# Two orders for the long and the short products in the FFN up-projection of a two-block transformer kernel

## The reference

```python
D_MODEL = 2048; SEQ = 256; D_FF = 5632; CONV_WIDTH = 3

def conv_ffn(h, w_up, conv_w, conv_b, w_down):
    B, S, _ = h.shape
    up = h @ w_up                      # [256, 2048] @ [2048, 11264]
    up_p = jnp.pad(up, ((0, 0), (CONV_WIDTH - 1, 0), (0, 0)))
    c = conv_b + sum(conv_w[j] * up_p[:, j:j + S] for j in range(CONV_WIDTH))
    gate, val = jnp.split(c, 2, axis=-1)
    return (jax.nn.silu(gate) * val) @ w_down

def reference(x, ...):
    x = first_block(x, ...)            # ends with x + conv_ffn(rmsnorm(x, ffn_norm_g), ...)
    return second_block(x, ...)
```

## Time and profile before

| | |
|---|---|
| time, median of 3 runs | 2346.7 us (2346.58 to 2346.95) |
| the profiled execution, its own time | 2346.09 us |
| its span, first to last instruction | 2343.8 us |
| TensorE matmul busy | 2329.4 us, 11,306 matmuls |
| TensorE weight load busy | 1944.9 us, 11,306 loads |
| DVE, ACT, POOL busy | 1527.5, 1134.4, 48.4 us |
| mean granted TensorE clock | 0.998 |
| HBM read | 431 MB, 185 GB/s over the span |

### The profile page before, as it was taken

One profiled execution on the slowest core, in us unless ns is written; L12 is line 12 of the kernel. 1 busy time (PEld: TensorE's weight loads), 2 busy tenths in 40 slices (PEclk: granted clock), 3 DMA queues, 4 the chain that ended last, 5 costly groups with the idle time before them and its releaser, 6 DMA issues.

```text
span 2343.8 us, 31449 instructions
## 1 busy us (share of the span) xinstructions
PE 2329.4 (99%) x11306; PEld 1944.9 (83%) x11306; DVE 1527.5 (65%) x1937; ACT 1134.4 (48%) x1418; POOL 48.4 (2%) x61
## 2 busy tenths in 40 slices
PE   9999999999999999999999999999999999999998
PEld 8788888888888888888888888888888888888886
DVE  5567576867777777668656666677656456456557
ACT  6444545644445555544454444455444434444443
POOL 1000000000000000000100000000000000000000
PEclk9999999999999999999999999999999999999999
DMA  9556545555655555565699659955755655665644
GB/s 318 162 171 205 162 152 180 189 190 190 191 190 190 191 188 192 188 191 183 215 177 188 179 172 172 182 183 188 214 171 176 195 167 175 198 188 161 196 156 143
DMA packets 220441, 434.74 MB, mean 185 GB/s; under 512 B 13392, under 2 KB 13680, under 8 KB 219568
## 3 DMA queue, kind: packets, MB, share of 16 engines
q1 hardware_dynamic: 218256, 422.50, 60.8%
q0 software_dynamic: 1648, 10.50, 1.2%
q10 hardware_dynamic: 432, 0.30, 0.0%
HBM read 431.05 MB, written 2.11 MB: 185 GB/s over the span
## 4 chain that ended last, share of the span: by engine, by line
PE 98%; DVE 1%; ACT 0%; DMA 0%; issue 0%; SPq 0%; DVEq 0%; ACTq 0%
PE acc L530 77%; PE mix L530 19%; PE mix L602 0%; PE mix L680 0%; DMA raw<-in_w_in 0%; PE mix L946 0%; PE mix L968 0%; PE mix L696 0%; DVE w_lo L1541 0%; PE mix L711 0%; DVE res L1554 0%; ACT w_hi L1048 0%; DVE res L2245 0%; ACT heads L1048 0%; ACT y_hi L1048 0%
## 5 line engine op out<-in xcount | busy, mean ns | idle before, releaser
L1541 DVE TENSOR_TENSOR w_lo<-raw,w_hi 128x1024 fp32r<-128x1024 f32 x788 | 960.6, 1222 | 585.5 <-ACT w_hi L1048 580.9
L1048 ACT ACTIVATE w_hi<-raw 128x1024 fp32r<-128x1024 f32 (+1 forms) x793 | 836.4, 1057 | 821.4 <-PE acc L530 638.5
L530 PE MATMUL acc<-w_hi,x_both 128*128 128x512 f32 x3296 | 1059.3, 395 | 0.9 <-DVE w_lo L1541 0.6
L530 PEld LDWEIGHTS acc<-w_hi,x_both 128*128 128x128 f32 x3296 | 618.9, 188 | 133.7 <-issue 5.1
L530 PE MATMUL acc<-w_lo,x_both 128*128 128x512 f32 x1648 | 641.7, 389 | 0.0
L530 PEld LDWEIGHTS acc<-w_lo,x_both 128*128 128x128 f32 x1648 | 309.9, 188 | 62.4 <-issue 1.4
L530 PE MATMUL acc<-w_hi,y_hi 128*128 128x512 f32 x640 | 253.6, 396 | 2.2 <-DVE y_lo L1705 2.1
L530 PE MATMUL acc<-x_both,w_hi 128*128 128x512 f32 (+2 forms) x768 | 254.9, 385 | 0.0
L530 PE MATMUL acc<-w_hi,y_lo 128*128 128x512 f32 x640 | 249.4, 390 | 0.0
L530 PE MATMUL acc<-w_lo,y_hi 128*128 128x512 f32 x640 | 249.2, 389 | 0.0
L530 PE MATMUL mix<-x_both,w_hi 128*128 128x512 f32 x704 | 244.5, 394 | 0.0
(11 more groups left out here) (213 smaller groups left out, 1474.1 us busy)
## 6 DMA issues: line engine op xcount, KB each, us to landing
raw<-in_ret_w_in SPq DMA_DIRECT2D x192, 512.0 KB, 4.2
raw<-in_w_up SPq DMA_DIRECT2D x176, 512.0 KB, 3.6
raw<-in_fox_w_in SPq DMA_DIRECT2D x128, 512.0 KB, 5.4
raw<-in_w_down SPq DMA_DIRECT2D x88, 512.0 KB, 4.2
raw<-in_w_in SPq DMA_DIRECT2D x79, 512.0 KB, 3.6
raw<-in_ret_w_out SPq DMA_DIRECT2D x64, 512.0 KB, 3.8
raw<-in_w_out SPq DMA_DIRECT2D x32, 512.0 KB, 3.7
raw<-in_fox_w_out SPq DMA_DIRECT2D x32, 512.0 KB, 4.1
```

Source lines behind the costliest of these rows:

```text
L530: return nc.tensor.matmul(o, l, r, start=start, stop=stop)
L1048: return nc.scalar.activation(o, i_, f, **kw)
L1541: V.tensor_tensor(lo, raw[:, g.base % RAW, :], hi, ALU.subtract).then_inc(lo_done, 1)
```

## The change

In each half chunk the four long products are issued in a row and the four short ones in a row. In chunk 0, where the bank has to be opened by a long product, the long ones come first, in all other chunks the short ones. Within a row the order is tile by tile, and in a tile both groups. The last product of the half chunk, whatever its kind, is the one that carries the semaphore.

```diff
@@ -835,16 +835,16 @@
                         if c == 0:
                             for blk in free[half != FFN_B % 2]:
                                 block_out(pe, blk)
-                        for k in range(KC):
-                            kt = c * KC + k
-                            for f in (2 * half, 2 * half + 1):
-                                at = slice(k * COL + f * P, k * COL + (f + 1) * P)
-                                o = banks[:, f, :].rearrange("p (a s) -> p a s", a=2)
-                                if kt > 0:
-                                    mm(o[:, 0, :], w_lo[:, slot, at], x_hi[:, kt, :], False, False)
-                                done = mm(o, w_hi[:, slot, at], x_both[:, :, kt, :], kt == 0, kt == KT - 1)
-                                if kt == 0:
-                                    mm(o[:, 0, :], w_lo[:, slot, at], x_hi[:, kt, :], False, False)
+                        for long in ((True, False) if c == 0 else (False, True)):
+                            for k in range(KC):
+                                kt = c * KC + k
+                                for f in (2 * half, 2 * half + 1):
+                                    at = slice(k * COL + f * P, k * COL + (f + 1) * P)
+                                    o = banks[:, f, :].rearrange("p (a s) -> p a s", a=2)
+                                    if long:
+                                        done = mm(o, w_hi[:, slot, at], x_both[:, :, kt, :], kt == 0, kt == KT - 1)
+                                    else:
+                                        done = mm(o[:, 0, :], w_lo[:, slot, at], x_hi[:, kt, :], False, False)
                     done.then_inc(used, 1)
                     if build and c + 4 < 8:
                         xt(1, c + 4)
```

## The result

| | before | after |
|---|---|---|
| time, median of 18 runs each | 2346.68 us | 2351.28 us |
| lowest and highest | 2345.92, 2347.14 | 2350.70, 2351.89 |
| ratio | | 1.0020, 95% interval 1.0014 to 1.0027 |
| span of the profiled execution | 2343.8 us | 2349.0 us |

The change costs 4.6 us. The forecast was 2348.8, 2.1 us more than before, with a range up to 2356.1. The sign and the range held; the size was a little over double, and the point lies just at the bound of 0.2% (4.7 us).

The account below looks back on a forecast made before the run. TensorE, never waiting in the FFN, was taken to bound the kernel. 352 half chunks at 6 ns add 2.1 us to the 2346.7 median, giving 2348.8 us; whole range 2343.5 to 2356.1, own range 2346.7 to 2351.3.

Parts of the forecast that it names:

- What bounds it: FFN stretch: TensorE busy for all of 662.1 us, so each nanosecond between two products is a nanosecond of the kernel.
- That nothing else moves: Whole kernel: same products, loads, waits and DMAs; semaphore move and neighbours' different PSUM banks costed at nothing; down blocks stay 21.78 us.
- Short to short at 117, short to long at 115: Column blocks: three short-to-long distances of 115 ns become short to short at 117, adding 6 ns a half chunk.
- Long to long at 232: Column blocks: two-piece long products in a row stand 232 ns apart, as long to short did; ends 227 and 236.
- The sum: All 352 half chunks of the column blocks: 6 ns each, +2.1 us, all on the path.
- three-plus-three formula: Per half chunk of a column block: change is 3 x (LL - LS) + 3 x (SS - SL), LS 232, SL 115.
- my own case: Column blocks: +2.1 us, limited by the first chunk's 13 ns a half chunk; 0.60 together with "The order doesn't matter".
- every change of length disturbs: Column blocks: each run of four never settles, costing 27 ns a half chunk, +9.4 us, 2356.1 us; chance 0.27.
- loads fall behind: Runs of four shorts: 188 ns loads exceed the 115 ns distance; without overlap 219 ns a half chunk, +77 us; chance 0.02.
- like the down blocks: Column blocks: longs in a row go at 227, shorts stay 115, gaining 5.3 us, 2341.4; gain over 4.7 us 0.11.
- The order doesn't matter: Column blocks: each product costs its columns and a fixed 13.4 ns, so 2346.7 stays; 0.60 together with the own case.

Follow-up runs that it names:

- runs of two: Against the kernel before, each tile issues two short products, then two long ones (first tile long first); 2348.54 us, ratio 1.0008.
- runs of eight: The change's order with the second half of each chunk but first and last turned round: eight longs, then eight shorts in a row; 2349.51 us, ratio 1.0012.
- 384 columns in turn: Order of the kernel before, with the short product given 384 columns instead of 256, read from other data; 2438.72 us, one run.

## Why the prediction was right or wrong

*What bounds it.* Right. TensorE never waits in the stretch read, and what its products are apart is what the kernel takes: the column blocks grew by 4.4 us, the median by 4.6.

*That nothing else moves.* Right: no wait was added, the down blocks kept their time, and the banks, tried by themselves in the alternation, cost nothing.

*Short to short at 117, short to long at 115.* Mis-sized. In rows both are 118 to 119, and shorts alone settle at 120. The working took the distance before a long product as one that stays while its neighbours change. In fact the mean of a short record went from 277 to 281, 4 ns on all four distances of a half chunk, where I had 2 ns on three.

*Long to long at 232.* Right as a number (233.2), wrong as a reason. I took 232 as what the two-piece form costs; the run with long products alone shows 226.7 for it. The 233 is a disturbance that a run of shorts leaves behind and that five longs wear off. That it comes out near 232 is chance.

*The sum.* 6 ns a half chunk was forecast and 14 measured; this is the step that failed. The three-plus-three formula by neighbours gives 3 x 1.2 + 3 x 3.6 = 14 with the distances of the kernel after, but the edges it left alone moved too (228.7 for 232, 118.2 for 115), and the same sum by neighbours gave 22.38 us a block for runs of two, which took 22.31, and 22.46 for runs of eight, which took 22.35. The 14 ns are the mean over a block: its steady chunks lost 16 to 17 a half chunk, the first one hardly anything (2780 or 2804 ns a chunk, from 2797 or 2800). The measured rate is close to that of the first chunk, 26 ns in 16 products, which I had in hand and set as the limit of my own case; that the two agree may be luck, as nothing shows one cause for both. And 352 x 14 ns would be 4.9 us; the third block, slow before, took 0.15 us less.

*The rival "every change of length disturbs".* Its mechanism is what happened, at half its price: 27 ns a half chunk was worked out, 14 came. I had each of two changes cost 13. Against the settled prices the longs pay, behind the shorts, and the shorts pay nothing over their 120, often less. Against the kernel before it reads the other way round, as its uneven alternation already had the longs at 232 and the shorts at 115: a half chunk's four longs take 928 ns in both kernels, its four shorts 474 instead of 460. Its counter-argument, that the alternation has settled and so a period of eight may too, was where it went astray. The alternation has two rhythms, and the kernel before was in the slow one for its third column block (412.40, 22.58 us), plain to see in the chain.

*The rival "loads fall behind".* Out as a lag that piles up: 184 shorts in a block go at 120 each. That loads have a part in what a change of length costs, the run with half loads shows; the prediction had no term for it. The Trainium skill's rule in TensorE: Matmul & The Clock Gate, section Architectural detail, that a matmul can begin before its load completes, fits this trace, where a product's load begins 3 ns behind the start of the product ahead and takes 188 ns by its record, while the product itself starts 112 to 118 ns after a short one; in the run of shorts alone the loads take 192 and the products are 120 apart.

*The rival "like the down blocks".* Its first half is true, long ones alone go at 227. Four in a row are too few to get there, and with 120 for the shorts it would have brought nothing: 226.7 + 120 is 346.7.

*"The order doesn't matter", a fixed 13.4 ns for each product.* True of settled sequences only: one length in a row, or the alternation with 256 columns in its fast rhythm. The Trainium skill's section Back-to-back issue gap, on the same page, has 2.5 ns in place of the 13.3; the two kernels of one length measure 226.7 and 120 where it gives 215.8 and 109.2. The section itself calls this the gap of an isolated product, which the prediction left out, and for a stream with weight loads it has 131 ns at 512 columns, further off still from the 226.7 here. The measurement decides.

## What to carry to other kernels

Where TensorE is the bound and never waits, read the distance between products by kind and compare it with what each kind costs in a row by itself. If the mix already runs at that sum, as here (346.7), there is little to win by an order, and all those tried lost or drew; where it lies above, as with 384 columns in turn, another order can gain. Look at every block of the chain, not at a typical one: a single block with the same instructions and another time shows that the sequence has a second rhythm, and then a small edit that only moves the sequence into it can cost more than the one under study (long first in every tile, 6.7 us against 4.6).

## What the runs showed of the hardware that was not expected

- An alternation of 512 and 256 columns, each with its own load, holds one of two rhythms for whole blocks: 346.7 or 353.3 ns a pair, with the same instructions, banks and clock. Which one hangs on what stands ahead, and in one execution it repeats from pass to pass of the loop; each kernel was profiled once, so that it repeats from execution to execution is shown by the close total times alone. Why there are two was not found.
- Runs of 2, 4 and 8 cost 22.31, 22.44 and 22.35 us a block against 22.19 to 22.21 in turn: the cost is not in step with the number of changes, 32, 16 and 8 pairs of them in a block, but each run of shorts, with the longs behind it, costs 4, 15 and 20 ns over the settled prices.
- In a row, products cost 13.3 ns over their columns at 2.4 GHz, at 512 (226.7) and at 256 (120), in one piece or two.
- With loads of 64 columns instead of 128, the grouped order went from 350.8 to 343.3 ns a pair in its steady chunks.
